# LN2's scale and shift rows turned on TensorE in the first expert's up stage, and ring place 21 loaded when LN1 is through

## The reference

```python
h = layer_norm(ALPHA * h + mix, ln1_g, ln1_b)            # mix: two groups of attention heads, one in- and one out-projection
h = layer_norm(ALPHA * h + xatt, ln2_g, ln2_b)           # xatt: cross-attention into 256 memory tokens
h = layer_norm(ALPHA * h + moe_ffn(h), ln3_g, ln3_b)

def moe_ffn(xt):                                         # 32 experts, each token goes to 4
    top_val, top_idx = lax.top_k(xt @ w_router + b_router, 4)
    combine = softmax(top_val) spread over the 32 experts
    for e in range(32):
        hid = clamped_swiglu(xt @ w_mlp1[e] + b_mlp1[e])   # w_mlp1[e]: 1024 x 2048
        y = y + combine[:, e:e + 1] * (hid @ w_mlp2[e] + b_mlp2[e])   # w_mlp2[e]: 1024 x 1024
```

## Time and profile before

| | |
|---|---|
| median of 3 runs | 1135.61 us (1135.2 to 1135.63) |
| profiled execution | 1137.09 us, its span 1135.2 us |
| PE busy | 1084.9 us (96%) |
| DVE busy | 322.2 us (28%) |
| ACT busy | 228.6 us (20%) |
| moved by DMA | 446.74 MB, mean 394 GB/s |

### The profile page before, as it was taken

The page is one execution under the profiler, slowest core; times in us unless marked ns, Lnnn a source line. Parts: engine busy times, 40 slices in busy tenths (PEclk is TensorE's granted clock), DMA queues, the critical chain, the costliest instruction groups (busy, mean ns, idle before and its releaser), DMA issues.

```text
span 1135.2 us, 15726 instructions
## 1 busy us (share of the span) xinstructions
PE 1084.9 (96%) x6536; PEld 522.0 (46%) x6536; DVE 322.2 (28%) x733; ACT 228.6 (20%) x411; POOL 8.1 (1%) x14
## 2 busy tenths in 40 slices
PE   9999999989999999999999999999999999999996
PEld 6888899843333333343333333333333333334331
DVE  6987775581111111121111111111111111012112
ACT  5667565440000100010010000000000000001001
POOL 0000000000000000000000000000000000000000
PEclk9999999999999999999999999999999999999999
DMA  9866868699999999999999999999999999999996
GB/s 354 295 193 238 289 209 331 230 388 419 436 431 435 432 433 432 435 433 433 432 434 434 432 435 433 433 432 435 433 432 433 434 434 431 431 430 429 432 426 250
DMA packets 41728, 446.74 MB, mean 394 GB/s; under 512 B 4832, under 2 KB 5728, under 8 KB 25088
## 3 DMA queue, kind: packets, MB, share of 16 engines
q1 hardware_dynamic: 41408, 445.76, 94.0%
q10 hardware_dynamic: 288, 0.52, 0.1%
HBM read 445.22 MB, written 1.05 MB: 393 GB/s over the span
## 4 chain that ended last, share of the span: by engine, by line
PE 58%; DMA 35%; SPq 3%; DVE 3%; issue 1%; ACT 0%; DVEq 0%
DMA ring<-in_w_mlp 33%; PE bank L1155 23%; PE bank L1199 9%; PE bank L685 5%; PE bank L687 5%; PE bank L686 5%; PE bank L1057 4%; PE bank L1045 2%; DMA w_raw<-in_w_in 2%; SPq L609 1%; PE bank L1094 1%; SPq L488 1%; SPq L502 1%; PE bank L927 1%; PE bank L911 1%; PE bank L1113 1%
## 5 line engine op out<-in xcount | busy, mean ns | idle before, releaser
L1155 PE MATMUL bank<-ring,live 128*64 128x512 f32 x2048 | 468.2, 605 | 27.9 <-DMA ring<-in_w_mlp 27.7
L1155 PEld LDWEIGHTS bank<-ring,live 128*64 128x64 f32 x2048 | 143.8, 138 | 310.4 <-issue 286.0
L1199 PE MATMUL bank<-ring,live 128*64 128x512 f32 x992 | 220.8, 596 | 6.8 <-DMA ring<-in_w_mlp 6.8
L1919 DVE COPY live<-bank 128x256 f32<-128x256 f32 x32 | 13.6, 425 | 527.8 <-PE bank L1087 527.8
L1199 PEld LDWEIGHTS bank<-ring,live 128*64 128x64 f32 x992 | 70.8, 137 | 130.8 <-issue 122.6
L1517 ACT ACTIVATE live<-bank 128x512 f32<-128x512 f32 x31 | 18.5, 597 | 325.1 <-PE bank L1094 325.1
L1589 DVE TENSOR_TENSOR w_low<-w_raw,w_high 128x1024 fp32r<-128x1024 f32 x61 | 72.3, 1221 | 23.8 <-ACT w_high L1291 23.6
L2009 DVE TENSOR_SCALAR live<-bank 128x256 f32<-128x256 f32 x64 | 24.2, 420 | 193.1 <-PE bank L1155 193.1
L1291 ACT ACTIVATE w_high<-w_raw 128x1024 fp32r<-128x1024 f32 x61 | 63.1, 1059 | 34.7 <-PE bank L687 16.6
L1513 ACT ACTIVATE live<-live 128x512 f32<-128x512 f32 x32 | 20.3, 635 | 239.4 <-DVE live L2009 239.4
L1045 PEld LDWEIGHTS bank<-pick,live 128*128 128x128 bf16 x1488 | 52.0, 118 | 27.0 <-issue 27.0
(11 more groups left out here) (253 smaller groups left out, 859.2 us busy)
## 6 DMA issues: line engine op xcount, KB each, us to landing
ring<-in_w_mlp SPq DMA_DIRECT2D x73, 4096.0 KB, 47.1
ring<-in_w_mlp SPq DMA_DIRECT2D x34, 2048.0 KB, 49.2
ring<-in_w_mlp SPq DMA_DIRECT2D x22, 1024.0 KB, 11.0
w_raw<-in_w_in SPq DMA_DIRECT2D x21, 512.0 KB, 10.0
w_raw<-in_w_mem_kv SPq DMA_DIRECT2D x16, 512.0 KB, 4.9
w_raw<-in_w_mix_out SPq DMA_DIRECT2D x8, 512.0 KB, 5.4
w_raw<-in_w_mem_q SPq DMA_DIRECT2D x8, 512.0 KB, 3.9
w_raw<-in_w_mem_o SPq DMA_DIRECT2D x8, 512.0 KB, 6.0
```

The lines of the kernel that those rows point to most:

```text
L1155: mm = pe.matmul(up[j][64 * g:64 * g + SLOTS, :], x_e[:, k, :], columns(row, j, g), start=False, stop=(k == KC - 1))
L1199: mm = pe.matmul(to[64 * g:64 * g + SLOTS, :], stationary[:, P * c + 64 * u:P * c + 64 * u + SLOTS], slot(at)[:, col:col + 512], start=(u ...
```

## The change

LN2's two gain loads go away. Instead PE makes the gain and shift rows itself: a column of 128 values, read as if it were 128 equal columns, is turned against the identity, which gives 128 equal rows of 128 values. Four such turns fill one bank with half a row (512 values). There are four groups of four, `turn_gains(part, q)`, one behind each of k = 0, 1, 2, 3 of the first up stage: scale into banks 2 and 6, shift into banks 4 and 5. The values lie in the bank in the order of `token_cols`, so DVE reads them with a step of 128 floats, four at a time. DVE first scales all four pieces (`scale_tokens`), then shifts all four (`shift_tokens`); each waits for its group (`gains_turned`). Place 21, free of LN2's rows, is loaded when LN1 is through, where `load_gains` stood behind unit 56.

```diff
         first_half_in, piece_in = [sem(f"first_half_in{i}") for i in range(HALVES)], [sem(f"piece_in{i}") for i in range(HALVES)]
         up_used, down_used = sem("up_used"), sem("down_used")
         before_last_half_in, last_half_in = ([sem(f"{name}{u}") for u in range(2)] for name in ("before_last_half_in", "last_half_in"))
-        last_up_in = sem("last_up_in")
+        last_up_in, gains_turned = sem("last_up_in"), sem("gains_turned")
         hot_ready, hot_used = sem("hot_ready"), sem("hot_used")
         pick_ready, pick_w_ready = sem("pick_ready"), sem("pick_w_ready")
         gathered, x_e_ready = sem("gathered"), sem("x_e_ready")
...
             return turn_banks[c % 4][:, SLOTS * (c // 4):SLOTS * (c // 4 + 1)]
+        gain_banks = [[banks[2], banks[6]], [banks[4], banks[5]]]
         turn_banks = [banks[3], banks[7], banks[4], banks[5]]
         def high_at(u):
...
                 elif place in (13, 17, 19):
                     wait_unit_used(sp, 63)
                 elif place == 21:
-                    sp.wait_ge(ln_ready, 12)
+                    sp.wait_ge(ln_ready, 8)
             def load(e, k, at):
                 sp.dma_start(slot(at), expert_src(e, k)).then_inc(piece_in[at], 16)
...
                     for i in range(3):
                         sp.dma_start(bias_f[E * i:E * (i + 1), :], a["b_mlp1"][0]).then_inc(bias_in, 16)
                 if u == 56:
-                    sp.wait_ge(ln_ready, 8)
-                    load_gains(a["ln2_g"], a["ln2_b"])
+                    prefetch(21, 1)
                 if u in EARLY:
                     prefetch(EARLY[u])
                 if u == 59:
...
                 sp.wait_ge(used, quarter // 2 + 1)
                 part = slice(2048 * quarter, 2048 * (quarter + 1))
                 sp.dma_start(slot(0)[:, part], expert_src(2, 0)[:, part]).then_inc(landed, 16)
-            prefetch(21, 1)
             sp.wait_ge(up_used, 3)
             load_half(2, 1, 1, 0)
             sp.wait_ge(up_done, 1)
...
                 bank_for(pe, "Y", 0, 0)
                 for _ in range(KEPT_BUSY[wait]):
                     pe.matmul(banks[4][:, 0:P], ident_b[:, :], ident_b[:, :], start=True, stop=True)
+            def turn_gains(part, q):
+                if part == 0 and q == 0:
+                    pe.wait_ge(token_cols_in, 16)
+                    pe.wait_ge(drained[2], bank_jobs[2])
+                    pe.wait_ge(drained[6], bank_jobs[6])
+                elif part == 1 and q == 0:
+                    pe.wait_ge(x_odd, KC // 2)
+                    pe.wait_ge(x_e_ready, 1)
+                for i in range(4):
+                    c = 4 * q + i
+                    mm = pe.transpose(gain_banks[part][q][:, P * i:P * (i + 1)],
+                                      token_cols[:, part, c:c + 1].broadcast_to([P, P]), ident)
+                mm.then_inc(gains_turned, 1)
             def gather_first(t, i):
...
                         mm.then_inc(up_used if k < KC - 1 else up_done, 1)
                     elif first and k < 4:
                         mm.then_inc(first_used, 1)
+                    if first and k < 4:
+                        turn_gains(k // 2, k % 2)
                     if k == 1 and earlier is not None and earlier[0] is not None and not scatter_first:
                         scatter_two_ago()
                     if k == 1 and weights:
...
                     dve.scalar_tensor_tensor(out=x[:, halves[q]], in0=x[:, halves[q]], scalar=ln_s[:, n, 1:2],
                                              in1=gb[:, 1, halves[q]], op0=ALU.mult, op1=ALU.add).then_inc(ln_ready, 1)
-            def normalise(t, q):
-                x = h2[:, t, 512 * q:512 * (q + 1)]
-                step(dve.scalar_tensor_tensor(out=x, in0=x, scalar=ln_s[:, 4 + t, 1:2], in1=gb[:, 0, 512 * q:512 * (q + 1)],
+            def columns_of(t, q):
+                return h2[:, t, 512 * q:512 * (q + 1)].rearrange("p (m i) -> p m i", i=4)
+            def gain_rows(part, q):
+                dve.wait_ge(gains_turned, 2 * part + q + 1)
+                return gain_banks[part][q][:, :].rearrange("p (i m) -> p m i", i=4)
+            def scale_tokens(t, q):
+                x = columns_of(t, q)
+                step(dve.scalar_tensor_tensor(out=x, in0=x, scalar=ln_s[:, 4 + t, 1:2], in1=gain_rows(0, q),
                                               op0=ALU.mult, op1=ALU.mult))
-                dve.tensor_tensor(x, x, gb[:, 1, 512 * q:512 * (q + 1)], ALU.add).then_inc(ln_ready, 1)
+            def shift_tokens(t, q):
+                x = columns_of(t, q)
+                dve.tensor_tensor(x, x, gain_rows(1, q), ALU.add).then_inc(ln_ready, 1)
             def fixed_logits(t):
...
                     dve.wait_ge(gathered, 1)
                 dve.tensor_scalar(x_e[:, c, :], first_tokens(c), token_cols[:, 0, c:c + 1],
                                   token_cols[:, 1, c:c + 1], ALU.mult, ALU.add).then_inc(x_odd, 1)
-            dve.wait_ge(gb_in, 96)
+            for q in range(2):
+                for t in range(NT):
+                    scale_tokens(t, q)
             for t in range(NT):
                 for q in range(2):
-                    normalise(t, q)
+                    shift_tokens(t, q)
             wait_drained(dve, "rank", 1)
             step(dve.tensor_scalar(small[:, 9:10], small[:, 8:9], float(SLOTS), 1.0, ALU.is_gt, ALU.add))
```

## The result

The changed kernel takes 1140.53 us (median of 6, 1139.11 to 1142.47), the kernel before 1135.27 (median of 6, 1134.98 to 1135.63): a ratio of 1.0047, 95% interval 1.0034 to 1.006. I had forecast 1135.9, no change that can be told, with a range to 1138.7: the change is clearly slower, and outside the range.

The account below looks back on a forecast made before the run. The weight stream was taken to set the end; the megabyte's 2.4 us were nearly all given back through one late load, a net +0.3 us on the median 1135.61, so 1135.9 us, range 1133.7 to 1138.7.

Parts of the forecast that it names:

- the removed megabyte: Weight stream behind 241 us: 1 MB less, so every later landing could be 2.4 us earlier, the most to be won.
- A group of turns: PE in the first up stage: four turns add 0.60 us per group, bounds 0.44 to 0.90.
- The strided bank operands: DVE's LN2 operations reading banks with a step of 128 floats: 0.69 us each, upper bound 1.18.
- The last shift: DVE's last LN2 operation waits for the fourth group and ends at 247.9 us, 5.3 us later than before.
- The clock: PE idles 4.7 us ahead of expert 1's gather; its clock may fall, costing 0.7 us, bounds 0 and 1.7.
- what the delay costs: At expert 2's down slot load: stream moves by the larger of -2.4 and d - 5.7, so +0.3 us.
- The delay d: PE's lateness from expert 1's gather on: 5.3 + 0.7 = 6.0 us, bounds 4.8 and 8.1.
- The other loads have more room.: Loads other than expert 2's down slot don't limit; halves issued in the first up stage move by only 0.6 to 2.4 us.
- my bounds: Time a load needs before its first byte moves: 2.2 to 4.2 us, taken 2.7.
- The cushion itself: Expert 2's down slot load was issued 8.4 us before the load ahead landed; 5.7 us of that taken as free.
- My own extreme of +3.9 us: Worst case for the stream behind the down slot's load: 8.1 us of delay less 4.2 us free.
- the drained queue: Rival: the down slot's load finds the queue empty and restart costs 4.2 us; +2.8 us, 1138.4 us, chance 20%.

Follow-up runs that it names:

- experiments 5 and 6: 5: changed kernel, scale rows turned ahead of first up stage, shift groups behind k = 0, 1133.53 us; 6: kernel before without place 21's load, 1133.72 us.
- experiment 7: Kernel before with unread reductions on DVE behind LN2: two 1138.63 us, four 1141.28 us, four with PE kept busy by unread products 1139.67 us.
- the second pair of profiles: Both kernels run and profiled again without any edit: the kernel before 1135.56 us, the changed kernel 1141.46 us.
- two reductions: Kernel before with two unread reductions (2.4 us) on DVE behind LN2's last addition: 1138.63 us.
- experiment 4: Changed kernel with two groups of turns behind each of k = 0 and 1, instead of one behind each of k = 0 to 3: 1136.34 us.

## Why the prediction was wrong

**What held.** The stream of weights sets the end, the removed megabyte is worth 2.0 to 2.2 us (experiments 5 and 6; I had 2.4), and the late gather gives it back. A group of turns adds 0.58 us to a k step, I had 0.60. The strided bank operands cost what dense ones from SBUF do: 684 ns for a shift (692 before) and 747 for a scaling (745 before); for the scalings I had 0.69, which did no harm, as they lie between the groups. The last shift ends 5.2 us later, I had 5.3. The clock fell in and behind the idle, and the gather took 1.0 us more: I had taken 0.7. The down slot's load was issued at 284.9, I had 284.8; there was some luck in that, since this execution's first up stage began 0.4 us early, and counted from it the load was 6.5 us late, not 6.0. The 390 ns that the Trainium skill's "VectorE: DVE Perf Modes", section on the three transpose paths, gives for one 128 x 128 turn of bfloat16 on PE is no price for turns in a row: four of float32 took 0.65 us here.

**The step that failed: what the delay costs.** I let the stream move by the larger of -2.4 us and d - 5.7, as if 5.7 us of delay were free and the rest were paid once, at the load with the smallest cushion. The delay d was nearly right (6.0, measured 6.5); its price was not. Measured were 5.3 us where I had 0.3, and in experiment 7 a load that was 3.5 us late already went with a loss of 2.9. Three things were wrong.

- *"The other loads have more room."* I priced the halves of the first up stage and forgot expert 3's four halves, which are issued in expert 1's up stage, behind the gather, and so move by the whole delay. The first of them had a cushion of 9.9 us before, and in the changed kernel it is issued 1.1 us after the queue has run empty. The megabyte accounts for 2.4 us of that and the delay for 6.2; the other 2.4 is that what was issued ahead had landed 4.8 us earlier (263.3 and 268.1), not 2.4. In the second pair of profiles it is 7.8 us of cushion before and 1.7 us of empty queue after: 2.4 for the megabyte, 6.5 for the delay and only 0.6 more. The stream at 241 to 245 us goes with it, 291 GB/s before and 420 in the changed kernel, but the turns need not be the reason: with place 21 late and no turn at all it also ran at 401 in one execution of experiment 7 (four reductions, PE kept busy), and at 367 in the second one of before:

```profile
241.00:245.00 4.00, 4.00 (x22) 1.66 (x20) 3.93 (x5) 1.22 (x2) 0.00 (x0) 1.00 1.01 401
```

- *The price is paid more than once.* The load at 264.4 took 3.8 us beyond its bytes, inside my bounds. But the two 4 MB loads behind it, with 2.6 and 3.4 us, lost 0.7 and 1.2 us more, and 0.2 and 2.5 in the second profile. A maximum over the loads has no room for such losses; they add up.
- *The cushion itself.* 8.4 us was read in one execution; in the second profile it is 6.3. With that number my own formula gives 6.0 - 3.6 = +2.4 us, or 1138.0 us: at the edge of what can be told, and still 2.5 us under the result. The larger error is in what I read. A load raises its semaphore in sixteen steps, the trace keeps the time of each, and "landed" is the last of them. At the load ahead of the down slot's the last step comes 2.7 us behind the middle one (between the eighth and the ninth) in the first profile of before and 1.2 in the second. By the middle step the cushion is 5.7 and 5.2 us, nearly the same in both. The part called "Open" shows that about 3 us of this must stay. By that estimate some 2 us were free, not 5.7, and the saved megabyte alone uses them up.

My own extreme of +3.9 us would have been 1139.5, above the 1138.7 at which I ended the range; the result lies beyond both.

Of the rivals, "the drained queue" came true. I had its place four loads too late (the down slot's load at 284.9, where the queue runs dry ahead of 264.4), its price too small, and its chance at 20%.

In the second pair of profiles the 6.1 us can be laid out. The load at 266.2 lands at 274.7, where its counterpart landed at 272.0: 2.7 us. At the load ahead of the down slot's the difference is 3.4 (289.96 and 286.56), the down slot's load adds 0.2 and the load at 296.2 adds 2.5 (12.2 us against 9.7).

**Open.** By the last landing the same cushion costs different amounts: 3.3 us cost 0.2 in the second profile, 3.0 cost 1.7 with two reductions, and 5.6 still cost 1.6 in experiment 4, while 5.0 cost 0.1 or nothing in experiments 5 and 6. The middle one of the sixteen steps puts this in order. Of the 4 MB loads issued from 278 to 300 us in the fourteen profiles, the 18 that had 1.2 to 2.8 us up to the middle step of the load ahead lost 0.3 to 1.4 us each (middle step to middle step, beyond 9.66 us). The 15 that had 3.3 us or more lost at most 0.3, and nearly all of them 0.1 or nothing. The 5.6 us of experiment 4 are 2.8 by this reading, because there the last step came 2.8 us behind the middle; the 5.0 of experiments 5 and 6 are 3.3 and 3.6. Why a load needs some 3 us of queue ahead of it, why the amount lost doesn't follow the cushion below that, and why one step lags isn't settled. Nor is it known why the stream is thin at 241 to 245 us in some executions.

## What to carry to other kernels

When a stream of loads sets the end, an engine's slack isn't a single number: for each load behind the edit write down when it is issued and when the one ahead lands, and move both by the edit. A load issued too close behind the landing of the one ahead loses time, an empty queue isn't needed for that, and the loads behind it lose again. A byte saved ahead of such a point is worth nothing until the lateness is gone; here moving eight turns ahead of the stage, and the other eight behind k = 0, turned a loss of 5.3 us into a gain of 2.2. Take the cushion from more than one execution, and not from the last landing alone, before you subtract it from anything.

## What the hardware showed that I had not expected

- 2 MB issued 1.1 and 1.7 us after the queue had run empty took 8.6 us to land, 3.8 beyond their bytes, in the two profiles of the changed kernel; 1 MB into an empty queue at 204.8 us had taken 2.2 beyond its bytes.
- With the idle of 6.77 us ahead of the gather (four reductions, PE not kept busy) the granted clock was at 0.50 (1.2 GHz) from 252.5 to 262 us, in most of the idle and at the start of the stage behind it (a line of PE's timeline, then the stretches):

```profile
256.88 2.72 PE L1045 MATMUL bank<-pick,live 128*128 128x64 bf16 x48 [6.77 <-DVE live L1919]
```

```profile
252.50:258.00 5.50, 1.12 (x22) 1.15 (x23) 3.73 (x11) 3.85 (x4) 0.00 (x0) 0.50 1.04 444
258.00:262.00 4.00, 4.00 (x38) 2.18 (x37) 2.39 (x7) 1.23 (x2) 0.00 (x0) 0.50 0.99 422
```

With PE kept busy the whole kernel took 1.6 us less (1139.67 against 1141.28), again with overlapping intervals.
- Eight float32 turns took 1.06 us in a row, 0.13 us each.
